# A decoder block on one core: one ring of weight tiles for three stages, adaLN columns in another order, subtractions moved to GpSimd, the merge's first splits moved into the delta rule

## What is computed

```
mod = silu(c) @ w_ada + b_ada                      # 6 x 1024: shift, scale, gate, twice
h   = rmsnorm(x, norm_pre_mix) * (1 + sc1) + sh1
proj = h @ w_in                                    # conv b, c, x; q, k, v, z; a, b; two gates
br_sc = (sc_b * causal_dwconv(sc_c * sc_x, sc_conv_w)) @ w_sc_out
q, k, v = split(silu(causal_dwconv([dn_q, dn_k, dn_v], dn_conv_w)))
q = l2norm(q) * DK ** -0.5 ; k = l2norm(k)
o = gated_delta_rule(q, k, v, g, beta)             # chunks of 64, 8 heads
br_dn = (rmsnorm(o, dn_out_norm) * silu(z)) @ w_dn_out
y = (sigmoid(gate_sc) * br_sc + sigmoid(gate_dn) * br_dn) @ w_mix_out
x = x + gt1 * rmsnorm(y, norm_post_mix)
h = rmsnorm(x, norm_pre_ffn) * (1 + sc2) + sh2
x = x + gt2 * rmsnorm(peer(h, ...), norm_post_ffn)
```

## Time and profile before

| what | value |
|---|---|
| median of three runs | 1945.85 us (1945.83 to 1947.31) |
| the profiled execution, its own time | 1948.68 us |
| its span | 1946.8 us |
| TensorE busy | 1786.5 us (92%) |
| VectorE busy | 1339.8 us (69%) |
| ScalarE busy | 701.2 us (36%) |
| GpSimd busy | 757.5 us (39%) |
| mean granted clock of TensorE | 0.965 |
| project stage | 0 to 180 us |
| delta stage | 180 to 407 us |
| merge stage | 407 to 617 us |

### The profile page before, as it was taken

One profiled execution on the slowest core, in us unless ns is written; L12 is line 12 of the kernel. 1 busy time (PEld: TensorE's weight loads), 2 busy tenths in 40 slices (PEclk: granted clock), 3 DMA queues, 4 the chain that ended last, 5 costly groups with the idle time before them and its releaser, 6 DMA issues. The chain is left out here.

```text
span 1946.8 us, 31281 instructions
## 1 busy us (share of the span) xinstructions
PE 1786.5 (92%) x11421; PEld 1570.5 (81%) x11421; DVE 1339.8 (69%) x2857; ACT 701.2 (36%) x1041; POOL 757.5 (39%) x443
## 2 busy tenths in 40 slices
PE   2899899979995998999998999979999999999997
PEld 1566777868874787999998999969998888888886
DVE  4783555543323467878776999967787888777776
ACT  3432223333314323333333445433333333333333
POOL 0332233214432345777772333313455443333330
PEclk9898999989997999999998999989999999999999
DMA  7672010013322226888885999998789999988983
GB/s 256 228 256 87 24 35 13 2 55 97 97 87 101 73 87 205 291 291 285 290 280 173 304 313 302 312 315 287 262 326 331 360 370 368 328 322 317 327 319 114
DMA packets 178681, 432.51 MB, mean 222 GB/s; under 512 B 15752, under 2 KB 91656, under 8 KB 178464
## 3 DMA queue, kind: packets, MB, share of 16 engines
q1 hardware_dynamic: 125088, 273.71, 42.1%
q0 software_dynamic: 36864, 134.23, 19.2%
q10 hardware_dynamic: 16640, 23.36, 3.3%
HBM read 383.54 MB, written 47.71 MB: 222 GB/s over the span
## 5 line engine op out<-in xcount | busy, mean ns | idle before, releaser
L198 POOL DMA_INDIRECT own_rows<-in_peer_v_dram,own_row x128 | 214.4, 1675 | 328.7 <-DVE y_own L1888 310.0
L1384 POOL TENSOR_TENSOR piece_lo<-v_tile,piece_hi 128x1024 fp32r<-128x1024 f32 x84 | 202.0, 2405 | 153.8 <-ACT piece_hi L1314 153.7
L198 POOL DMA_INDIRECT own_rows<-in_u_rows_dram,own_row x128 | 161.8, 1264 | 246.9 <-DVE own_rows L1601 185.4
L1245 PE MATMUL bank<-h_hi,piece_hi 128*128 128x384 f32 (+1 forms) x672 | 237.2, 353 | 13.8 <-DVE h_lo L1490 7.0
L1245 PE MATMUL bank<-h_lo,piece_hi 128*128 128x384 f32 (+1 forms) x672 | 234.9, 350 | 0.0
L1245 PE MATMUL bank<-h_hi,piece_lo 128*128 128x384 f32 (+1 forms) x672 | 234.9, 350 | 0.0
L1798 PE MATMUL bank<-v_hi,coef_lo 128*128 128x512 f32 x512 | 199.7, 390 | 0.0
L1798 PE MATMUL bank<-v_lo,coef_hi 128*128 128x512 f32 x512 | 199.6, 390 | 0.0
L1798 PE MATMUL bank<-v_hi,coef_hi 128*128 128x512 f32 x512 | 199.2, 389 | 0.1
L1314 ACT ACTIVATE piece_hi<-v_tile 128x1024 fp32r<-128x1024 f32 x84 | 89.3, 1063 | 254.2 <-PE bank L1245 244.9
L1873 DVE TENSOR_TENSOR v_lo<-v_tile,v_hi 128x1024 fp32r<-128x1024 f32 x128 | 156.5, 1223 | 24.7 <-ACT v_hi L1829 22.8
(11 more groups left out here) (399 smaller groups left out, 4255.8 us busy)
## 6 DMA issues: line engine op xcount, KB each, us to landing
v_tile<-in_peer_v_dram SPq DMA_DIRECT2D x128, 512.0 KB, 5.3
v_tile<-in_peer_u_dram SPq DMA_DIRECT2D x68, 512.0 KB, 4.8
ada<-in_w_ada_dram SPq DMA_DIRECT2D x48, 512.0 KB, 5.2
gate_scratch<-gate_block SPq DMA_DIRECT2D x48, 512.0 KB, 6.5
gate_tiles<-gate_scratch SPq DMA_DIRECT2D x32, 768.0 KB, 6.8
gelu_scratch<-gelu_early ACTq DMA_DIRECT2D x104, 192.0 KB, 4.6
gelu<-gelu_scratch SPq DMA_DIRECT2D x104, 192.0 KB, 5.3
u_early<-in_peer_u_dram SPq DMA_DIRECT2D x36, 512.0 KB, 5.4
```

The costliest lines, as they stand in the source:

```text
L198: pool.indirect_dma_start(own_rows[:, n % R], None, tables[n // NS], bass.IndirectOffsetOnAxis(ap=own_row[:, n % NS:n % NS + 1], axis=0)). ...
L1245: last = nc.tensor.matmul(out, ww[:, n % HR, k, :], x[:, k, 0:nt], start=(k == 0 and m == 0), stop=(k == KT - 1 and m == 2))
L1384: nc.gpsimd.tensor_tensor(w_lo[:, n % HR], w[:, n % WR], w_hi[:, n % HR].bitcast(F32), ALU.subtract).then_inc(lo_ready, 1)
```

## The change

- One ring of four weight tiles, `weight_ring`, is allocated for the whole program. The project, delta and merge stages use it with one running count of tiles, and the later stages use it as `v_tile`. The buffers of high and low parts and their semaphores live through the first three stages.
- `project_stage`: AR is 8 in place of 6 (the room comes from laying `h_raw`, `sq` and `sel16` over `scT` and `row_ffn`). x has a semaphore per tile, and each square waits for its own. On ScalarE's queue the constants come second, and six small loads go behind the silu. VectorE makes columns 0 to 3 and the first shift and scale, columns 4 and 5, then the reciprocal and `xn`, then the other columns; the eight subtractions for `h_lo` are GpSimd's, in front of and around the first weight tile's. ScalarE's second split goes behind the last k-tile. Root and reciprocal of the squared sums are at n == 9.
- `delta_stage`: SyncE loads the merge's tiles 0 to 3; ScalarE and GpSimd split merge tiles 0 and 1 in the last token tile.
- `merge_stage`: TensorE's product loop is written out for its four rounds. It begins with tiles 0 and 1, the diagonal matmuls stand behind tile 1, and tile 2 waits for `br_lo1`. The last weight tile is multiplied by itself, and each bank's end is signalled there.

The diff, cut to its core:

```
-    AR, K2 = 6, 2
+    AR, K2 = 8, 2
...
-        h_raw = sb(ctx, "h_raw1", [P, 2, T])
+        h_raw = g["scT"][:, 2:4, :]
...
+                def rest(n):
                     pool.wait_ge(hi_ready, n + 1)
                     nc.gpsimd.tensor_tensor(w_lo[:, n % 2], wring[:, n % WRING], w_hi[:, n % 2].bitcast(F32), ALU.subtract).then_inc(lo_ready, 1)
+
+                for k in range(KT):
+                    pool.wait_ge(*A.after(f"hi{k}"))
+                    nc.gpsimd.tensor_tensor(h_lo[:, k, :], h_raw[:, k % 2], h_hi[:, k, :].bitcast(F32), ALU.subtract).then_inc(h_low, 1)
+                    if k == KT - 3:
+                        rest(0)
+                for n in range(1, N_HERE + 2):
+                    rest(n)
...
+                for dst, name in small[3:]:
+                    act.dma_start(dst, a[name]).then_inc(s_small, 16)
                 act.wait_ge(s_wab, 16)
                 nc.scalar.activation(wab_hi, w_ab[:], ACT.Copy).then_inc(ab_hi, 1)
-                act.wait_ge(s_x, 16 * TT)
                 for t in range(TT):
+                    act.wait_ge(s_x[t], 16)
...
-                    if n == 10:
+                    if n == 9:
                         act.wait_ge(ss_done, 8)
...
                         mod_column(n)
+                        if n == 5:
+                            dve.wait_ge(*A.after("std"))
+                            nc.vector.reciprocal(stat[:, 2, :], stat[:, 1, :]).then_inc(*V.step("rstd"))
...
-                    for j in range(k, k + K2):
-                        dve.wait_ge(*A.after(f"hi{j}"))
-                        nc.vector.tensor_tensor(h_lo[:, j, :], h_raw[:, j % 2], h_hi[:, j, :].bitcast(F32), ALU.subtract).then_inc(*V.step(f"lo{j}"))
...
-                    if n == 10:
+                    if n == 9:
                         dve.wait_ge(norm_done, 1)
...
-                for n in range(N0 + WRING, N_PROJ):
+                for n in range(N0 + WRING, N_PROJ + WRING):
                     sp.wait_ge(lo_ready, n - WRING + 1)
...
-                with pe.Fori(0, n_loop) as i:
+                for i in range(n_loop):
                     for b in range(2):
-                        pe.wait_ge(*V.after(f"dn{b}", i, 1))
+                        if i:
+                            pe.wait_ge(*V.after(f"dn{b}", i, 1))
...
+                            if i == 0 and m == 1:
+                                rows()
...
-                for k in range(KT - 2):
-                    pe.wait_ge(lo_ready, NM + k + 1)
+                for k in range(KT):
+                    pe.wait_ge(lo_ready, B + NM + k + 1)
...
-                for t, half in outs:
-                    mix(KT - 2, 0, t, half, False, False)
-                    mix(KT - 1, 1, t, half, False, True).then_inc(*E2.step(f"y{half}_{t}"))
```

More of the change, by code:

```diff
@@ L201, in program @@
             env["fetch"] = fetch
-            env["v_tile"] = sb(late, "v_tile", [P, G, D])
+            env["v_tile"] = ring
             env["u_tile"] = sb(late, "u_tile", [P, 2, KT, P])
@@ L689, in _ @@
                     rest(3 * tt + 3)
+                rest(3 * TT + 1)
             @block.tensor
@@ L1054, in _, with split @@
+                for b in range(2, WRING):
+                    rest(b, B + b + 1)
+                with pool.Fori(1, NW // WRING) as i:
+                    for b in range(WRING):
+                        rest(b, i * WRING + (B + b + 1))
             @block.scalar
             def _(act):
-                def split(b, landed):
-                    act.wait_ge(s_m[b], landed)
-                    nc.scalar.activation(w_hi[:, b], wm[:, b], ACT.Copy).then_inc(hi_ready, 1)
-                for b in range(2):
-                    split(b, 16)
+                def split(m):
+                    n = B + m
+                    act.wait_ge(s_w[n % WRING], 16 * (n // WRING) + 16)
+                    nc.scalar.activation(w_hi[:, n % 2], wring[:, n % WRING], ACT.Copy).then_inc(hi_ready, 1)
@@ L1063, in _, with rows @@
                 for n, x in enumerate((scT, oT)):
                     nc.scalar.activation(br_hi[:, n], x[:], ACT.Copy).then_inc(br_ready, 1)
-                for n in range(4):
-                    act.wait_ge(*E0.after(f"row{n}"))
-                    dst = (row_mix, row_ffn)[n // 2]
-                    nc.scalar.activation(dst[:, 512 * (n % 2):512 * (n % 2) + 512], bank[4 + n][:], ACT.Copy).then_inc(*A0.step(f"row{n}"))
-                with act.Fori(0, n_loop) as i:
+                def rows():
+                    for n in range(4):
+                        act.wait_ge(*E0.after(f"row{n}"))
+                        dst = (row_mix, row_ffn)[n // 2]
+                        nc.scalar.activation(dst[:, 512 * (n % 2):512 * (n % 2) + 512], bank[4 + n][:], ACT.Copy).then_inc(*A0.step(f"row{n}"))
@@ L1070, in _ @@
+                for i in range(n_loop):
                     for m in range(6):
                         b, n = m // 3, m % 3
[L1072 to L1073 removed]
+                        act.wait_ge(piece_done, B + i * 6 + m + 1)
+                        split(i * 6 + m + 2)
                         if n < 2:
[L1075 removed]
+                            if i:
+                                act.wait_ge(*V.after(f"dn{b}", i, 1))
@@ L1076, in _ @@
                             nc.scalar.activation(sg[:, b, n, :], bank[4 * b + n][:], ACT.Sigmoid).then_inc(sg_ready, 1)
-                with act.Fori(0, KT // 2 - 1) as i:
-                    for b in range(2):
-                        act.wait_ge(piece_done, i * 2 + (NM + b + 1))
-                        split(b, i * 16 + 8 * NM + 32)
+                        if i == 0 and m == 1:
+                            rows()
+                for k in range(KT - 2):
+                    act.wait_ge(piece_done, B + NM + k + 1)
+                    split(NM + k + 2)
```

117 lines of the change are left out of this document (55 added, 62 removed).

## The result

The changed kernel takes 1924.23 us (median of four runs, 1921.38 to 1926.24), the kernel before 1946.58 us beside it. The ratio is 0.9879, 95% interval 0.9856 to 0.9901: faster by 22 to 24 us, where 24.5 were forecast. Four more runs, later, gave 1921.99 us (1917.17 to 1924.18) and 0.9869 (0.9854 to 0.9885). The profiled execution took 1922.71 us with a span of 1920.9, against 1948.68 and 1946.8 before, 26 us less.

A forecast was written before the change was run, and what follows sets the result against it. TensorE was taken to set the end of the first three stages, idling at stage starts and a few waits. Gains of 15.3 + 6.0 + 1.2 + 2.0 = 24.5 us gave 1921.3 us at the median, range 1915 to 1928.

The forecast's parts named there:

- part 3: Delta rule to merge: earlier splits and two early tiles, yet VectorE's order holds tile 2; 1.2 us won, -1 to +3.4.
- Part 1: Projection start: early squares, reordered VectorE queue, subtractions on GpSimd; tile 0 at 46.3 for 61.6, 15.3 us won, 12 to 18.
- Part 2: Projection: reciprocal of squared sums one tile earlier removes TensorE's wait before the spreads; 6.0 us won, 4 to 6.6.
- The charge for the held tiny operations: Projection start: VectorE's tiny operations wait for GpSimd's instructions; 0.6 us before scale 2, 2.3 before scale 6.
- the 5 us of the estimate: Projection start: by the skill's engine rule, eight subtractions on GpSimd take twice as long, adding some 5 us.
- the 1.0 us for the clock: Merge tile 2: about 1.0 us lost to the clock, because TensorE idled ahead of it.
- Part 4: Merge's end: last tile taken by itself, so TensorE does not wait for its low part; 2.0 us won, 1 to 2.5.
- rival 1: GpSimd holds VectorE more than charged, at the start or merge; up to 8 us back, 1927 to 1930; chance 0.12.
- rival 2: Projection start: loads do not keep up, its gain only 9 to 12 us, time 1925 to 1928; chance 0.08.
- rival 4: Projection start: x or a small load late, VectorE stands until 24 us, time 1933; chance 0.05.
- rival 3: Merge's two early tiles are real, br_lo not held by row 1; first matmul 14.4 us earlier, 1908; chance 0.04.
- rival 5: Merge's unrolled product loop makes TensorE wait for instructions; five stalls cost 30 us, about 1951; chance 0.03.

The follow-up runs named there:

- Run 6: Changed kernel with GpSimd's low part of weight tile 0 moved behind all eight of h; 1922.71 us, ratio 0.9864.
- run 3: Changed kernel with six ada slots in place of eight; 1921.67 us, ratio 0.9872.
- run 2: Changed kernel with the eight h_lo subtractions on VectorE, one pair of k-tiles later, in place of GpSimd; 1922.83 us, ratio 0.9866.
- run 5: Changed kernel with a second buffer for the merge's second diagonal and no wait for row 1; 1916.92 us, again 1914.76 us.
- run 7: Changed kernel with the merge's diagonal matmuls ahead of tile 0, as in the kernel before (rows first); 1917.6 us, again 1920.68 us.
- run 8: Changed kernel with the merge's last two weight tiles multiplied together, bank by bank, as before; 1925.54 us, ratio 0.9888.

## Why the prediction was right, and where not

The forecast of 1921.3 us lies 2.9 below the first median and 0.7 below the second. Its four parts made 24.5 us, the profiles' milestones 24.9 at the merge's end. The mechanisms were right; that the sum comes so close is partly luck, as part 3 won 1.5 more than forecast, while parts 1 and 2 won 0.8 less and the delta rule took 0.2 more. The 1.0 us behind the merge stands in no part. One sum of the forecast is off: its bounds add up to 16 to 30.5 us, that is 1915 to 1930 us, and not to 1928.

**Part 1, 15.3 forecast, 14.9 measured.** xn came at 22.6 (22.3 forecast), scale 6 at 41.0 (40.9), tile 0 at 46.7 (46.3). The charge for the held tiny operations was right in kind and near in sum: 0.7 before scale 4 and 1.8 before scale 6, 2.5 in all, where I had 0.6 before scale 2 and 2.3. Run 6 shows its cause. What was wrong is the part that I gave the eight slots in keeping the loads ahead: with six, tile 0 starts at the same time (run 3). And the move to GpSimd, which I treated as what frees VectorE, matters by 1.0 us (run 2). The Trainium skill ("GPSIMD Engine Reference", "Engine selection") would leave such work to VectorE, since GpSimd is about twice as slow with two inputs; the trace agrees on the factor, 1.285 us on GpSimd against 0.69 on VectorE. Still the move did not cost the 5 us of the estimate but won 1.0 (run 2), as GpSimd subtracts beside VectorE's columns.

**Part 2, 6.0 forecast, 7.1 measured at tile 13 and 5.6 at tile 14.** Of the difference 0.9 lies ahead of the spreads: counted from tile 0 they start at 76.4 us, where the earlier trace rows and the wait give 77.2. Of this, 0.4 is there by the end of tile 0, which in the kernel before ran at the low clock for 2.0 us in place of 1.2; the rest builds up in small steps over the tiles behind, without a wait, and is not explained. Another 0.3 is the wait before the second spreads, 0.17 in place of 0.5. Then the clock fell in tile 13, which the forecast had no term for.

**Part 3, 1.2 forecast, 2.7 measured.** The merge's first matmul was due at 408.2 in the time of before and came at 387.83 + 20.3 = 408.1; diag 1 was due at 426.8 and came at 426.4; tile 2 at 431.4 and came at 430.9. The mis-sized term is the 1.0 us for the clock: TensorE idled only 0.87 us ahead of tile 2, the granted clock was 1.00 in the first 10 us of it, and its first 24 matmuls took 5.6 us in place of 5.4. The other 0.5 is the chain itself, a little quicker than counted. The step that VectorE's order eats the early tiles is shown by run 5, which takes that order away and wins 5.9 us. What I did not say, and run 7 shows in its two profiles: with the weights in place the old order brings tile 2 nearer by 1.4 and 3.4 us.

**Part 4, 2.0 forecast, 1.9 measured** (24.9 less 23.0), and 2.2 in run 8.

**The rivals.** Columns stayed at 1.22 us; they waited for loads up to column 4, at 19.9, and for none behind it (column 5 followed at 21.2, in time for the forecast), which excludes rivals 1, 2 and 4. Tile 2 excludes rival 3 (14 us), and run 5 shows what would have been in it: 5.9. Nothing speaks for rival 5: TensorE has one wait in the merge's products, 2.8 us for the last merged low part, and it had that before as well.

**What I left out** is that time won ahead of the delta rule is not carried through it one to one. Its length was 221.9 to 228.7 us in 13 profiles of the change and its variants, with the same work. Part of it is TensorE's clock: by its windows it was low for 22 us of the stage in the two profiles of 221.9 us, and for 27 to 32 in the other eleven. But between the two profiles of run 7, where the stage took 6.6 us more, TensorE's busy time grew by 3.9 and its idle time by 2.7, so the clock's direct cost is not all of it.

## What to carry to other kernels

Before moving an operation to another engine, see whether its queue is slow because of work or because it stands and waits for an input: one pair later on the same engine gave all but 1 us of what the move gave. When tiles are pulled forward on one engine, follow the short chain that their successor needs (here gate, diagonal, row, low part) through every engine: if a link of it stands behind the tiles, the tiles replace idle time ahead of them with idle time behind them, and a second small buffer was worth more than the whole reordering (5.9 us against 2.7 at tile 2). And measure such steps at milestones in the profile, as the total moves by several us with the clock.

## What the hardware did that I had not expected

TensorE's granted clock fell to 1.2 GHz with no wait to explain it. Ahead of 133.1 us in the changed kernel TensorE had issued matmuls for 10 us with one wait of 0.17 us; four spreads, on 16 rows, ended just before the fall. The same place in the two executions of rows first (windows on TensorE: busy, granted clock, DMA share, GB/s), first

```profile
134.00:137.40 3.40, 3.40 (x16) 1.00 0.42 110
```

then

```profile
134.00:137.40 3.40, 3.40 (x11) 0.60 0.63 218
```

In one it stayed at 2.4 GHz, in the other it was low for most of 3.4 us. It fell there in six of the twelve profiles of kernels with the norm at n == 9, and not in the other six. In the six with the fall the first spreads had started at 122.58 to 123.16 us, in the others at 122.48 or at 123.46 and later. So it seems to hang on when the spreads come, within less than a microsecond, but no run moved them on purpose, and what decides it stays open. I had charged the low clock only behind waits.
